# Attention value products over groups of two neighbouring query blocks, six probability places, scores two groups ahead

## Chip, core and metric

The kernel runs on one core of a Trainium2 chip (trn2). The metric is the device time of the whole program in microseconds (us), the median of three runs. The engines of a core run side by side and meet at semaphores: TensorE (PE) multiplies into PSUM, VectorE (DVE), ScalarE (ACT) and GpSimd (POOL) work element by element, SyncE (SP) issues DMAs.

## What is computed

One layer of a decoder trunk on 1024 tokens of width 1024, all float32. Four causal attention branches (A windowed, B dilated, C top-k, D forgetting), eight heads of 64 each, run on one input; each is projected, gated and summed, an output projection and a LayerNorm follow, then a convolutional gated FFN. The change lies in the attention proper, which in every branch has this form:

```python
s = einsum('bqhd,bshd->bhqs', q, k) * hd ** -0.5 + bias   # bias, slopes and masks differ by branch
p = softmax(where(causal, s, NEG_INF), axis=-1)           # branch A: a sink logit joins the denominator
o = einsum('bhqs,bshd->bqhd', p, v)
x = layer_norm(alpha * x + sum_branches(gate * proj(o)) @ w_out)
x = layer_norm(alpha * x + (gelu(conv(x @ w_up)) * (x @ w_ffn_gate)) @ w_down)
```

## The kernel before

Products are kept accurate by splitting an operand into a high and a low part (`hi`, `lo`, type fp32r), so a projection is three matmuls of 128x512 for each tile of weights and a value product is two (`pt_hi`, `pt_lo`).

The branches run in the order B, A, C, D, each as four pairs of heads. In a pair, 16 **units** (one head, one block of 128 queries) go through one chain. Unit (e, i) has i+1 key blocks of 128 (in A at most two). The chain of a unit is:

1. PE `scores`: two matmuls per piece of up to 512 columns into one of two `pair` buffers.
2. DVE `biased`: adds the bias, writes the probability place `prob_slot`, and takes the row's extreme.
3. ACT `exps`: exponential in place, with the row sum; in A one more small exponential for the sink.
4. DVE `inverse`: reciprocal of the sum (in A an addition before it).
5. POOL: scales the place by it.
6. PE `transposes`: 128x128 each, up to four into one of two `chunk` buffers; ACT `pt_hi`, then DVE `pt_lo` copy the chunk out as two parts, and free it.
7. PE `values`: for each key block two matmuls of 128 columns (the stationary operand is the block of v, the moving one the transposed probabilities), added up in a bank of `obank`; four units fill a bank, and ACT and DVE copy it out (`outputs`).

The order is written out by hand on every engine, by one loop over the units: at step u, PE does scores of unit u+2, transposes of u-1 and values of u-2; ACT does `pt` of u-2 and then `exps` of u; DVE `pt` of u-2, `biased` of u+1, `inverse` of u. `UNIT_ORDER` mixes long and short units. There are four probability places.

The **filler** is the projection of the next pair (q and k in B and D, q alone in A and C, the first gate tile of the merge at a branch's last pair). It is cut into parts of six matmuls, and PE takes parts of it only in the last five steps of a pair (u of 13 and more), between transposes and values; what is left follows after the loop. In A and C the next pair's q then goes through `place_q` (two ACT and two DVE instructions on 1024 columns) before its first scores (`chain`). In B, D and the first pair of A, v of the pair itself is projected ahead of the loop (`beside_v`): the first two units' scores run in that time, v is transposed, and ACT and DVE copy it out (`v_hi`, `v_lo`).

POOL also makes the low parts of weight tiles (`split_weights`, L1050), and up to two of them stand inside a pair, behind units 8 and 12.

Of the kernel before, what the change touches and what calls it, by code (L numbers as in the profile page):

```python
# [16 lines left out]
P = 128  # L43
# [38 lines left out]
PROB_SLOTS = 4  # L82
# [26 lines left out]
UNIT_ORDER = [(0, 0), (0, 1), (0, 2), (1, 7), (0, 3), (1, 6), (0, 4), (1, 5), (0, 5), (1, 4), (0, 6), (1, 3), (0, 7), (1, 2), (1, 1), (1, 0)]  # L109
# [16 lines left out]

_groups = [(e, i // 4) for e, i in UNIT_ORDER]
BANK_OF = [sorted(set(_groups), key=_groups.index).index(g) for g in _groups]  # L130
# [9 lines left out]
def begun(br, pr):  # L140


    return 2 if beside_v(br, pr) else 1 if pr > 0 else 0


def chunk_bases(br, pr, start):


    out = []
    for u, unit in enumerate(units_of(br, pr)):  # L150
        out.append(start)
        start += len(pieces(unit[4])) + (2 if u == 0 and beside_v(br, pr) else 0)
    return out
# [31 lines left out]
def build_layer(nc, x, w_in, b_forget, sinks, w_branch, w_gate, b_gate, w_out, ln1_g, ln1_b,  # L185
# [10 lines left out]
    with ctx:  # L196
# [11 lines left out]
        stat = sb("stat", [P, 64])  # L208

# [4 lines left out]
        prob = sb("prob", [P, PROB_SLOTS - 1, SEQ], F32, mixer)  # L214
        pt_hi = sb("pt_hi", [P, PT_SLOTS, HALF], F32R, mixer)
        pt_lo = sb("pt_lo", [P, PT_SLOTS, HALF], F32R, mixer)
        bias = sb("bias", [P, SEQ], F32, mixer)
        dist = sb("dist", [P, SEQ], F32, mixer)
# [89 lines left out]
        def prob_slot(br, u):  # L308

            k = u % PROB_SLOTS  # L310
            if k < PROB_SLOTS - 1:
                return prob[:, k, :]
            return {A: bias[:, HALF:SEQ], B: mid[:, 4, :], C: bias[:, :], D: score[:, 0:SEQ]}[br]
# [74 lines left out]
        def _(pe):  # L388
# [77 lines left out]
            def attention(br, pr, filler):  # L466
                units = units_of(br, pr)
                chain = br in (A, C) and pr < PAIRS - 1

                def transposes(u):  # L470
                    n = units[u][4]
                    pe.wait_ge(prob_ready, probs.next())
                    for s, m in pieces(n):
                        t = next_chunk()
                        for j in range(m // P):
                            last = nc.tensor.transpose(t[:, j * P:(j + 1) * P],  # L476
                                                       prob_slot(br, u)[:, s + j * P:s + (j + 1) * P], ident[:])
                        last.then_inc(chunk_full, 1)

                def values(u):  # L480
                    h, e, i, k0, n = units[u]
                    kv = {A: h // 4, C: 0}.get(br, e)
                    if BANK_EDGE[u][0]:
# [3 lines left out]
                    dst = obank[BANK_OF[u] % 2][:, (i % 4) * P:(i % 4 + 1) * P]  # L487
                    nkb = n // P
                    for s, m in pieces(n):
                        c = pvs.next() - 1  # L490
                        pe.wait_ge(chunk_free, chunk_base[u] + s // HALF + 1)
                        for j in range(m // P):
                            kb = s // P + j
                            v = v_view1[:, k0 + kb, :] if br == C else v_view[:, k0 + kb, kv, :]
                            for w, part in enumerate((pt_hi, pt_lo)):
                                last = nc.tensor.matmul(dst, v, part[:, c % PT_SLOTS, j * P:(j + 1) * P],  # L496
                                                        start=(kb == 0 and w == 0),
                                                        stop=(kb == nkb - 1 and w == 1))
                        if s + m < n or not BANK_EDGE[u][1]:
                            last.then_inc(pv_used, 1)  # L500
                        else:
                            last.then_inc(obank_full, 1)
# [7 lines left out]
                if beside_v(br, pr):  # L510
                    scores(br, pr, 2)
                    transposes(0)
                    pe.wait_ge(pair_free, pairs.n - 1)
                    transpose_tokens(staged)
                elif pr == 0:
                    pe.wait_ge(pair_free, pairs.n)
                    scores(br, pr, 0)
                    scores(br, pr, 1)
                n_units = len(units)
                for u in range(n_units + 2):  # L520
                    if u + 2 < n_units and not (u == 0 and beside_v(br, pr)):
                        scores(br, pr, u + 2)
                    draining = (2 if chain else 1) if u >= n_units - 3 else 0
                    if 1 + beside_v(br, pr) <= u <= n_units:
                        transposes(u - 1)
                    fill(draining)
                    if u == 2:
                        pe.wait_ge(chunk_free, chunk_base[1])
                    if u == n_units and chain:
# [3 lines left out]
                    if u >= 2:  # L533
                        values(u - 2)
# [223 lines left out]
        def _(act):  # L758
# [55 lines left out]
            def exps(br, pr, u):  # L814
# [3 lines left out]
                else:  # L818
                    act.wait_ge(pair_free, pairs.next())
                last = nc.scalar.activation(prob_slot(br, u)[:, 0:n], prob_slot(br, u)[:, 0:n], ACT.Exp,  # L820
                                            bias=stat[:, u % 4:u % 4 + 1], scale=-1.0,
                                            accum_out=stat[:, 4 + u % 4:5 + u % 4])
                if br == A:
# [11 lines left out]
            def attention(br, pr):  # L835
# [12 lines left out]
                def outputs(u):  # L848
                    if not BANK_EDGE[u][1]:
                        return  # L850
# [748 lines left out]
```

## Time and profile before

| | before |
|---|---|
| median of 3 runs | 2539.01 us (2538.95 to 2539.84) |
| profiled execution, span from first to last instruction | 2535.9 us |
| four pairs of B, first to last value product | 260.6 us |
| four pairs of A | 165.9 us |
| four pairs of C | 205.6 us |
| four pairs of D | 259.7 us |

The span and the median differ by 3.1 us, which lies around the first and last instruction. In the rows below a group of instructions reads: line, engine, operation, what it writes and reads, shape, count, then busy us, mean ns of one, idle time before. A timeline row reads: start, duration, engine, line, operation, and in brackets the idle time before it and who ended it. PE's durations overlap, so the time that a matmul takes from the stream is the distance of its start to the next one's start.

### The profile page before, as it was taken

The page shows a single profiled execution, that of the slowest core. Times are in us where ns is not written, and L with a number is a line of the kernel's source. Part 1 is how long each engine was busy: PE and PEld are TensorE (multiplying, and loading weights), DVE is VectorE, ACT ScalarE, POOL GpSimd, SP SyncE. Part 2 cuts the span into 40 slices and gives each one's busy share as a digit, 9 for nine tenths or more (in the row PEclk, how much of TensorE's full clock was granted, in tenths as well). Part 3 has the DMA queues.
Part 4 walks back from the last instruction along what each step waited for, and adds up shares of the span by engine and source line. Part 5 has one row for each costly group of instructions (what it writes and reads, how often), then busy time and mean ns, then how long its engine had stood idle before and what let it go on. Part 6 is the DMA issues. An engine that isn't in the chain of part 4 may idle for free. (4 is left out here: it accounts for less than half of the span.)

```text
span 2535.9 us, 30015 instructions
## 1 busy us (share of the span) xinstructions
PE 2352.2 (93%) x11696; PEld 1962.3 (77%) x11696; DVE 1231.5 (49%) x2359; ACT 868.9 (34%) x1533; POOL 629.8 (25%) x472
## 2 busy tenths in 40 slices
PE   7799999997889979899999999989999999999996
PEld 5488788786777767788888888868888888878775
DVE  3576556876568884551255553155211111134653
ACT  3355444125441144551155543232211112222331
POOL 1032222212212222222223222330122222224333
PEclk9799999998789989899999999999999999999998
DMA  3200001110001100001211001240111111123223
GB/s 108 19 26 17 18 22 38 40 52 17 13 18 46 50 15 7 9 18 50 71 34 42 26 23 54 79 137 1 42 45 47 50 50 51 50 67 100 86 88 108
DMA packets 165965, 116.33 MB, mean 46 GB/s; under 512 B 22456, under 2 KB 154552, under 8 KB 165824
## 3 DMA queue, kind: packets, MB, share of 16 engines
q1 hardware_dynamic: 149632, 112.21, 14.9%
q10 hardware_dynamic: 16192, 2.20, 0.6%
q8 instruction: 93, 1.52, 0.3%
q14 instruction: 48, 0.39, 0.1%
HBM read 110.17 MB, written 4.23 MB: 45 GB/s over the span
## 5 line engine op out<-in xcount | busy, mean ns | idle before, releaser
L1050 POOL TENSOR_TENSOR w_lo<-w_raw,w_hi 128x1024 fp32r<-128x1024 f32 (+1 forms) x190 | 425.3, 2239 | 1245.6 <-ACT w_hi L772 1245.6
L428 PE MATMUL pair<-act_hi,w_hi 128*128 128x512 f32 x1824 | 722.9, 396 | 12.4 <-DVE act_lo L1331 6.9
L428 PE MATMUL pair<-act_lo,w_hi 128*128 128x512 f32 x1824 | 713.3, 391 | 0.0
L428 PE MATMUL pair<-act_hi,w_lo 128*128 128x512 f32 x1824 | 713.1, 391 | 0.0
L772 ACT ACTIVATE w_hi<-w_raw 128x1024 fp32r<-128x1024 f32 (+1 forms) x190 | 187.3, 986 | 885.6 <-PE pair L428 703.5
L428 PEld LDWEIGHTS pair<-act_hi,w_hi 128*128 128x128 f32 x1824 | 344.5, 189 | 84.8 <-issue 8.5
L428 PEld LDWEIGHTS pair<-act_hi,w_lo 128*128 128x128 f32 x1824 | 344.2, 189 | 73.2
L428 PEld LDWEIGHTS pair<-act_lo,w_hi 128*128 128x128 f32 x1824 | 344.8, 189 | 67.4
L1273 DVE TENSOR_TENSOR pt_lo<-chunk,pt_hi 128x512 fp32r<-128x512 f32 (+3 forms) x352 | 182.0, 529 | 192.8 <-ACT pt_hi L792 189.8
L496 PE MATMUL obank<-pt_hi,heads 128*128 128x128 f32 x984 | 247.2, 288 | 5.8 <-DVE pt_lo L1273 5.7
L1079 POOL TENSOR_SCALAR prob<-prob,stat 128x896 f32<-128x896 f32 (+2 forms) x192 | 128.8, 671 | 471.9 <-DVE stat L1252 471.0
L496 PE MATMUL obank<-pt_lo,heads 128*128 128x128 f32 x984 | 243.9, 285 | 0.0
L792 ACT ACTIVATE pt_hi<-chunk 128x512 fp32r<-128x512 f32 (+3 forms) x352 | 161.4, 468 | 221.5 <-PE chunk L476 188.3
L451 PE MATMUL pair<-heads 128*128 128x512 f32 (+3 forms) x374 | 158.8, 425 | 54.9 <-DVE stat L1239 18.8
L496 PEld LDWEIGHTS obank<-pt_hi,heads 128*128 128x128 f32 x984 | 197.2, 200 | 12.9 <-DVE pt_lo L1273 8.0
L496 PEld LDWEIGHTS obank<-pt_lo,heads 128*128 128x128 f32 x984 | 198.1, 201 | 2.6
L1511 DVE SCALAR_TENSOR_TENSOR conv_s<-pair,convw,conv_s 128x1023 f32<-128x1023 f32 (+1 forms) x44 | 56.4, 1283 | 260.1 <-ACT conv_s L792 259.4
L428 PE MATMUL pair<-heads,w_hi 128*128 128x512 f32 x512 | 159.6, 393 | 13.3 <-DVE heads L1331 5.7
L1144 DVE TENSOR_SCALAR_CACHE_REDUCE o_top<-score,stat 128x640 uint8<-128x640 f32 (+3 forms) x182 | 162.2, 949 | 9.5 <-issue 8.4
L820 ACT ACTIVATE prob<-prob,stat 128x896 f32<-128x896 f32 (+2 forms) x192 | 133.4, 695 | 61.5 <-DVE stat L1239 60.8
L451 PEld LDWEIGHTS pair<-heads 128*128 128x128 f32 x374 | 82.3, 220 | 77.9 <-DVE stat L1239 26.6
L452 PE MATMUL pair<-heads 128*128 128x512 f32 (+3 forms) x374 | 137.6, 379 | 0.0
(190 smaller groups left out, 2958.5 us busy)
## 6 DMA issues: line engine op xcount, KB each, us to landing
w_raw<-in_w_down SPq DMA_DIRECT2D x44, 512.0 KB, 3.6
w_raw<-in_w_in SPq DMA_DIRECT2D x37, 512.0 KB, 3.8
w_raw<-in_w_gate SPq DMA_DIRECT2D x32, 512.0 KB, 4.1
w_raw<-in_w_up SPq DMA_DIRECT2D x22, 512.0 KB, 3.9
w_raw<-in_w_ffn_gate SPq DMA_DIRECT2D x22, 512.0 KB, 3.8
mid<-in_x SPq DMA_DIRECT2D x16, 512.0 KB, 6.7
w_raw<-in_w_branch SPq DMA_DIRECT2D x32, 256.0 KB, 2.8
w_raw<-in_w_out SPq DMA_DIRECT2D x8, 512.0 KB, 3.5
```

Of the source, the lines that this page charges most:

```text
L428: last = nc.tensor.matmul(dst[0:cols, s:s + HALF], w[:, k, :], a[:, k, s:s + HALF], start=(k == 0 and n == 0), stop=(k == kt - 1 and n == 2))
L451: nc.tensor.matmul(dst[:, s:s + m], q, k_hi[:, s:s + m], start=True, stop=False)
L452: last = nc.tensor.matmul(dst[:, s:s + m], q, k_lo[:, s:s + m], start=False, stop=not masked)
L496: last = nc.tensor.matmul(dst, v, part[:, c % PT_SLOTS, j * P:(j + 1) * P], start=(kb == 0 and w == 0), stop=(kb == nkb - 1 and w == 1))
L772: nc.scalar.activation(split_into(0, g), w_raw[:, g % 2, 0:kt * cols], ACT.Copy).then_inc(hi_ready, 1)
L792: nc.scalar.activation(dst, src, func, **kw).then_inc(act_part, 1)
L820: last = nc.scalar.activation(prob_slot(br, u)[:, 0:n], prob_slot(br, u)[:, 0:n], ACT.Exp, bias=stat[:, u % 4:u % 4 + 1], scale=-1.0, accu ...
L1050: nc.gpsimd.tensor_tensor(split_into(1, g), w_raw[:, g % 2, 0:kt * cols], split_into(0, g).bitcast(F32), ALU.subtract).then_inc(lo_ready, 1)
L1079: nc.gpsimd.tensor_scalar(prob_slot(step[1], u)[:, 0:n], prob_slot(step[1], u)[:, 0:n], stat[:, 12 + u % 4:13 + u % 4], 1.0, ALU.mult, ALU ...
L1144: nc.vector.tensor_scalar(junk[topk_where[0]][:, b % 2, 0:(i + 1) * P], s, limit if isinstance(limit, float) else limit[:, b:b + 1], None, ...
L1273: nc.vector.tensor_tensor(pt_lo[:, c % PT_SLOTS, 0:m], t[:, 0:m], pt_hi[:, c % PT_SLOTS, 0:m].bitcast(F32), ALU.subtract).then_inc(chunk_f ...
L1511: ins = nc.vector.scalar_tensor_tensor(conv_s[:, back:SEQ], src[:, 0:SEQ - back], convw[:, NCONV - 1 - back, ft:ft + 1], conv_s[:, back:SE ...
```

## The change

The 16 units become eight **groups** of two neighbouring query blocks 2m and 2m+1 of one head, in the order of `GROUPS`. One step g of the loop is now one chunk of a group. A chunk of B, C and D holds two key blocks for both query blocks (512 columns), and a group's last one 384; a group has m+1 chunks. In A every group has one chunk. The moving operand of a value product is 256 columns where both query blocks see the key block, and 128 for the last one (in A for two of the three). `exps` signals, and `inverse` and the first transposes wait, once for a group, that is for both its units. Scores of group j+2 go ahead at the first chunk of group j. Probability places are six, taken from spare memory (`aux`, `mid`, `score`). The filler starts with the seventh group (`j >= NGROUPS - 2`). POOL's splits still stand behind units 8 and 12.

```diff
-UNIT_ORDER = [(0, 0), (0, 1), (0, 2), (1, 7), (0, 3), (1, 6), (0, 4), (1, 5), (0, 5), (1, 4), (0, 6), (1, 3), (0, 7), (1, 2), (1, 1), (1, 0)]
+GROUPS = [(0, 0), (0, 1), (0, 2), (0, 3), (1, 2), (1, 1), (1, 3), (1, 0)]
+NGROUPS = len(GROUPS)
+UNIT_ORDER = [(e, 2 * m + w) for e, m in GROUPS for w in range(2)]
...
+def group_chunks(branch, j):
+
+    m = GROUPS[j][1]
+    if branch == A:
+        return [[(2 * m, (0, 1))] + [(2 * m - 1, (0,))] * (m > 0) + [(2 * m + 1, (1,))]]
+    blocks = [(kb, (0, 1)) for kb in range(2 * m + 1)] + [(2 * m + 1, (1,))]
+    return [blocks[c:c + 2] for c in range(0, len(blocks), 2)]
...
+                for g in range(len(stream) + 2):
+                    j, c = stream[g] if g < len(stream) else (NGROUPS, 1)
+                    ahead = c == 0 and j + 2 < NGROUPS
+                    draining = (2 if chain else 1) if j >= NGROUPS - 2 else 0
+                    if ahead:
+                        scores(br, pr, 2 * j + 4)
+                    if j < NGROUPS and not (g == 0 and beside_v(br, pr)):
+                        transposes(j, c)
                     fill(draining)
+                    if ahead:
+                        scores(br, pr, 2 * j + 5)
...
+                    if g >= 2:
+                        values(*stream[g - 2])
                     fill(draining)
```

ACT and DVE in the loop:

```diff
 # ACT
+                    if j < NGROUPS and not (g == 0 and beside_v(br, pr)):
+                        pt(j, c)
+                    if second is not None:
+                        exps(br, pr, second)
+                        second = None
+                    if c == 0 and j + 2 < NGROUPS:
+                        exps(br, pr, 2 * j + 4)
+                        second = 2 * j + 5
 # DVE
+                    if ahead:
+                        biased(br, pr, 2 * j + 4, chunk_base)
+                    if j < NGROUPS and not (g == 0 and beside_v(br, pr)):
+                        pt(j, c)
+                    if waiting is not None:
+                        inverse(br, waiting)
+                        waiting = None
+                    if ahead:
+                        biased(br, pr, 2 * j + 5, chunk_base)
+                        waiting = j + 2
 # POOL
+                        if u % 2 == 0:
+                            pool.wait_ge(rsum_ready, sums.next())
...
                         if u in (8, 12) and ring.n < needed + 2:
                             split_weights()
```

What stands in a row on POOL at the end of a pair of B, before (the scalings of units 11 and 12, a weight tile's low part, the scalings of 13 to 15):

```order
L1079 TENSOR_SCALAR mid<-mid,stat 128x512
L1079 TENSOR_SCALAR prob<-prob,stat 128x1024
L1050 TENSOR_TENSOR w_lo<-w_raw,w_hi 128x1024
L1079 TENSOR_SCALAR prob<-prob,stat 128x384
L1079 TENSOR_SCALAR prob<-prob,stat 128x256
L1079 TENSOR_SCALAR mid<-mid,stat 128x128
```

And in the changed kernel (units 10 and 11, unit 12, the low part, unit 13, units 14 and 15):

```order
L1112 TENSOR_SCALAR mid<-mid,att 128x384
L1112 TENSOR_SCALAR mid<-mid,att 128x512
L1112 TENSOR_SCALAR prob<-prob,att 128x896
L1082 TENSOR_TENSOR w_lo<-w_raw,w_hi 128x1024
L1112 TENSOR_SCALAR prob<-prob,att 128x1024
L1112 TENSOR_SCALAR mid<-mid,att 128x128
L1112 TENSOR_SCALAR prob<-prob,att 128x256
```

The low part stood between two units; it now stands between the two halves of the seventh group, of which PE's next transposes need both.

On ACT in the middle of a pair of A, before (`pt_hi` of a unit, exponential and sink of the unit two further):

```order
L792 ACTIVATE pt_hi<-chunk 128x256 [waits pv_used,chunk_full]
L820 ACTIVATE bias,stat<-bias,stat 128x256 [waits pair_free]
L824 ACTIVATE stat<-sink,stat 128x1
L792 ACTIVATE pt_hi<-chunk 128x256 [waits obank_full,chunk_full]
L820 ACTIVATE prob,stat<-prob,stat 128x256 [waits pair_free]
```

And now (`pt_hi` of group j, the second exponential of group j+1 with the sink, the first of group j+2):

```order
L816 ACTIVATE pt_hi<-chunk 128x512 [waits obank_full,chunk_full]
L844 ACTIVATE prob,att<-prob,att 128x256 [waits pair_free]
L848 ACTIVATE att<-att,sink 128x2
L844 ACTIVATE prob,att<-prob,att 128x256 [waits pair_free]
L816 ACTIVATE pt_hi<-chunk 128x512 [waits obank_full,chunk_full]
```

The exponential that completes a group now stands behind the `pt_hi` of the group just ahead of it; before, one unit lay between them.

## Rows read from the trace of the kernel before

**Rows 1.** Page, busy us of each engine (share of the span) xinstructions

```profile
PE 2352.2 (93%) x11696; PEld 1962.3 (77%) x11696; DVE 1231.5 (49%) x2359; ACT 868.9 (34%) x1533; POOL 629.8 (25%) x472
```

**Rows 2.** Stages B, A, C, D: us, busy PE, PEld, DVE, ACT, POOL, PEclk, DMA, GB/s

```profile
155.10:415.70 260.60, 247.97 (x1549) 216.45 (x1548) 154.10 (x345) 133.49 (x269) 71.71 (x73) 0.99 0.08 21
579.70:745.60 165.90, 137.69 (x670) 117.23 (x669) 94.11 (x336) 83.60 (x275) 39.43 (x67) 0.77 0.05 14
919.00:1124.60 205.60, 188.46 (x1235) 166.55 (x1235) 118.79 (x302) 111.57 (x245) 57.48 (x67) 0.93 0.04 11
1285.70:1545.40 259.70, 251.02 (x1607) 216.61 (x1606) 142.06 (x331) 133.91 (x268) 71.77 (x73) 1.00 0.11 33
```

**Rows 3.** Groups by line and shape, whole span, the value products

```profile
L496 PE MATMUL obank<-pt_hi,heads 128*128 128x128 f32 x984 | 247.2, 288 | 5.8 <-DVE pt_lo L1273 5.7
```

**Rows 4.** Timeline of PE in a pair of B

```profile
162.66 0.28 PE L496 MATMUL obank<-pt_hi,heads 128*128 128x128 f32 x1
162.78 0.28 PE L496 MATMUL obank<-pt_lo,heads 128*128 128x128 f32 x1
...
163.17 0.39 PE L452 MATMUL pair<-heads 128*128 128x512 f32 x1
163.40 0.28 PE L451 MATMUL pair<-heads 128*128 128x256 f32 x1
163.51 0.28 PE L452 MATMUL pair<-heads 128*128 128x256 f32 x1
163.64 0.82 PE L476 MATMUL chunk<-ident,prob 128*128 128x128 f32 x6
```

**Rows 5.** Timeline at the start of a pair of B, behind v

```profile
224.63 1.29 DVE L1331 TENSOR_TENSOR heads<-chunk,heads 128x512 fp32r<-128x512 f32 x2 [1.25 <-ACT heads L792]
...
226.44 0.50 PE L451 MATMUL pair<-heads 128*128 128x512 f32 x1 [1.19 <-DVE stat L1239]
```

**Rows 6.** Timeline at the end of a pair of B, one long unit and the split

```profile
248.42 1.22 DVE L1239 CUSTOM_DVE_ANT_0 prob<-pair,bias 128x1024 f32<-128x1024 f32 x1
...
250.68 1.14 ACT L820 ACTIVATE prob<-prob,stat 128x1024 f32<-128x1024 f32 x1
...
252.20 1.12 POOL L1079 TENSOR_SCALAR prob<-prob,stat 128x1024 f32<-128x1024 f32 x1 [1.70 <-DVE stat L1252]
...
253.28 2.40 POOL L1050 TENSOR_TENSOR w_lo<-w_raw,w_hi 128x1024 fp32r<-128x1024 f32 x1
253.38 1.18 PE L476 MATMUL chunk<-ident,prob 128*128 128x128 f32 x8 [0.41 <-POOL prob L1079]
```

**Rows 7.** Timeline in a pair of A, one turn of the chain

```profile
637.07 0.44 PE L476 MATMUL chunk<-ident,prob 128*128 128x128 f32 x2 [1.99 <-POOL prob L1079]
...
637.55 0.38 ACT L792 ACTIVATE pt_hi<-chunk 128x256 fp32r<-128x256 f32 x1 [2.06 <-PE chunk L476]
...
637.83 0.50 ACT L820 ACTIVATE bias<-bias,stat 128x256 f32<-128x256 f32 x1
...
638.32 0.28 ACT L824 ACTIVATE stat<-sink,stat 128x1 f32<-128x1 f32 x1
...
639.22 0.48 POOL L1079 TENSOR_SCALAR bias<-bias,stat 128x256 f32<-128x256 f32 x1 [1.20 <-DVE stat L1252]
```

**Rows 8.** Stretch of a pair of A, first transposes to filler

```profile
622.30:642.00 19.70, 16.70 (x93) 14.35 (x92) 16.03 (x64) 13.70 (x51) 8.05 (x13) 0.76 0.05 14
```

**Rows 9.** Timeline in C, the next pair's q is placed

```profile
1014.84 2.06 ACT L792 ACTIVATE heads<-pair 64x1024 fp32r<-64x1024 f32 x2 [6.46 <-PE pair L428]
...
1018.47 0.28 PEld L451 LDWEIGHTS pair<-heads 128*128 128x128 f32 x1 [2.89 <-DVE heads L1260]
```

**Rows 10.** Stretch of a pair of C, first scores to filler

```profile
964.60:1000.40 35.80, 32.55 (x227) 29.08 (x228) 25.70 (x69) 22.75 (x53) 12.83 (x14) 0.90 0.03 9
```

**Rows 11.** Two stretches in B behind each other

```profile
293.90:297.30 3.40, 0.66 (x6) 0.66 (x7) 2.68 (x8) 0.81 (x2) 0.00 (x0) 1.00 0.00 0
297.30:300.70 3.40, 3.15 (x10) 2.14 (x9) 2.60 (x5) 1.90 (x4) 0.00 (x0) 0.50 0.00 0
```

More of the change, by code:

```diff
@@ L81 @@
 PT_SLOTS = 3
-PROB_SLOTS = 4
+PROB_SLOTS = 3
 V_PARTS, MERGE_PARTS, FIRST_PARTS = 2, 13, 9
@@ L140, in begun @@
 def begun(br, pr):
-    return 2 if beside_v(br, pr) else 1 if pr > 0 else 0
+    return 2 if beside_v(br, pr) or pr > 0 else 0
 def chunk_bases(br, pr, start):
     out = []
-    for u, unit in enumerate(units_of(br, pr)):
+    for j in range(NGROUPS):
         out.append(start)
-        start += len(pieces(unit[4])) + (2 if u == 0 and beside_v(br, pr) else 0)
+        start += len(group_chunks(br, j)) + (2 if j == 0 and beside_v(br, pr) else 0)
     return out
@@ L468, in attention, with transposes, values @@
                 chain = br in (A, C) and pr < PAIRS - 1
[L470 to L481, printed above, removed]
+                stream = chunk_stream(br)
+                def transposes(j, c):
+                    if c == 0:
+                        pe.wait_ge(prob_ready, probs.next(2))
+                    t = next_chunk()
+                    at = 0
+                    for kb, halves in group_chunks(br, j)[c]:
+                        for w in halves:
+                            s = (kb - units[2 * j + w][3]) * P
+                            last = nc.tensor.transpose(t[:, at:at + P], prob_slot(br, 2 * j + w)[:, s:s + P], ident[:])
+                            at += P
+                    last.then_inc(chunk_full, 1)
+                def values(j, c):
+                    h, e, i, k0, n = units[2 * j]
                     kv = {A: h // 4, C: 0}.get(br, e)
-                    if BANK_EDGE[u][0]:
+                    chunks_of = group_chunks(br, j)
+                    if c == 0 and BANK_EDGE[j][0]:
                         o = obanks.next() - 1
@@ L1305, in attention @@
                             biased(br, pr + 1, 0)
-                    if u == len(units) - 1 and br in (A, C) and pr < PAIRS - 1:
-                        place_q(br, pr + 1)
-                    if u >= 3:
-                        outputs(u - 3)
-                outputs(len(units) - 1)
+                            biased(br, pr + 1, 1)
+                            waiting = 0
+                    if g >= 3 and bank_closes(br, *stream[g - 3]):
+                        outputs(stream[g - 3][0])
             def make_bias(br, pr):
```

251 lines of the change are left out of this document (133 added, 118 removed).

## The prediction

> **What bounds the kernel now.** I read the page's busy times first, then the stretches of the four attention stages, then the timeline of a pair in each. PE is the bound nearly everywhere: it is busy 93% of the span, DVE 49%, ACT 34% [rows 1]. In the attention stages the distance is smaller. PE is busy 248 of 261 us in B, 251 of 260 in D, 188 of 206 in C, but 138 of 166 in A, where its clock is granted at 0.77 on average, while DVE has 94 and ACT 84 us to do [rows 2]. So B, C and D go by the length of PE's stream, and A partly by the chain between the engines. Two questions decide: how much shorter the stream gets, and what PE then waits for.
>
> **Part 1, wider value products.** In the stream a value product of 128 columns takes 0.11 us, start to start (162.66 to 162.78) [rows 4]; its duration in the group, 288 ns, overlaps with its neighbours. There are 984 of each part, 1968 in all [rows 3]: 144 in a pair of B, C or D, 60 in a pair of A. The trace has no value product of 256 columns, but a score product of 256 columns with weights of its own takes 0.11 to 0.13 us (163.40, 163.51, 163.64) [rows 4]; I take 0.12. A pair of B, C or D will have 64 such and 16 of 128 columns: 64 x 0.12 + 16 x 0.112 = 9.5 us in place of 144 x 0.112 = 16.1, so -6.6. A pair of A has 16 and 28: 5.1 in place of 6.7, so -1.6. Over twelve and four pairs that is **-86 us of PE's stream**. At 0.11 it would be -94, at 0.13 -78.
>
> Against this stands a rule of the Trainium skill (TensorE: Matmul & The Clock Gate, section on what overlaps and what doesn't): a weight load overlaps a running matmul only where their row groups differ, which they don't here. The trace disagrees for wide products: one of 512 columns takes 0.23 us (163.17 to 163.40) [rows 4], four times the 0.055 that is left of 0.11 once half of it is the load. By the rule a product of 256 would cost 0.055 + 0.11 = 0.17, and the -86 would be -44; that is a rival below.
>
> **Part 2, fewer and fuller chunks.** A pair of B, C or D has 20 chunks in place of 24, one of A 8 in place of 16, and half as many signals. DVE and ACT save about 1 us a pair each; they are not the bound by their sums (half of PE's in the stage), so I cost this at nothing by itself. It is in the walks below.
>
> **Part 3, the chain is now one of groups.** This is where the gain goes. I walked the changed order by hand, with each engine's instructions in a row at the durations of the trace. Eight blocks take DVE's bias 1.22, ACT's exponential 1.14 and POOL's scaling 1.12 us [rows 6], the sum's read-out 0.19 more; shorter ones proportionally less, over a fixed part of some 0.2; a full chunk 0.5 on ACT and 0.6 on DVE, a hop between engines about 0.1.
>
> *Start of a pair of B or D.* Now PE waits 1.2 us for the bias behind the copies of v [rows 5]. After, the scores of unit 5 need unit 3's bias, which stands behind the same copies: about 1.7. Then the second group needs both its units scaled (0.8 of waiting), and the third again (1.5: it waits for unit 5's exponential, its reciprocal, and two scalings of 0.8 and 0.9 in a row). In the middle about 1.5 more, in pieces, where a chunk buffer is still being copied.
>
> *Before the filler.* Now the split of a weight tile, 2.40 us on POOL, costs PE 0.41: the transposes of unit 12 run beside it [rows 6]. After, it stands between units 12 and 13, which the seventh group needs both. Unit 13's scores end at t; DVE's bias is ready at t + 1.9 (a chunk is ahead of it), the exponential at t + 3.1, the reciprocal at t + 3.3; POOL adds 0.1 + 1.0 + 2.4 + 1.1, so the transposes start at t + 8.0. PE has only 5.0 us of work until then, and the filler stands behind these transposes: **3.0 us of waiting**, of which 2.4 are the split.
>
> Sum for such a pair: -6.6, and waits of 8.5 in place of 2.6, so -0.7; by absolute times of the walk -1.0, which I take. At a branch's last pair the filler is over with the eighth group's first chunk to come, and the copy of the outputs, 3 us on ACT, stands ahead of the last two banks: +1. Six pairs at -1 and two at +1: **-4**. If none of the new waits came, it would be -53; if each were half as long again, +19.
>
> *C.* The walk from a pair's first scores to the filler gives 31.1 us (14.1 to the third group's transposes, 17.0 from there; in C POOL has one split, not two) in place of 35.8 [rows 10]. But the filler of q is over two steps into the seventh group, and `place_q` stands behind the eighth group's `pt` on ACT; its 3.6 us from ACT's start to the next scores [rows 9] then have 0.5 us of PE's work beside them. From the filler's start to the next scores it is 19.4 in place of 18.1 (1018.47 [rows 9] less 1000.40 [rows 10]). **-3.4 for three pairs, -1 for the last: -11.**
>
> *A.* Every group has one chunk, so the chain closes on itself: PE transposes group j, ACT copies it, *then* runs the last exponential and the sink of group j+1, DVE adds and inverts, POOL scales two units, PE transposes j+1. From the timeline [rows 7]: first transpose to ACT 0.48 plus two more transposes 0.22; a full chunk 0.50; exponential to sink 0.49; sink 0.28; sink's end to POOL 0.62 (639.22 less 638.60) of which 0.1 is DVE's queue; two scalings 0.94; PE 0.06. That is **3.5 us for a group**. Now the same loop goes over two units, 2.9 us, with one scaling and a shorter copy: twelve units and the split take 19.7 us with the first step of filler [rows 8]. After, six groups take 6 x 3.5 + 2.4 = 23.4. PE's 1.6 us are saved beside it, where they are worth nothing. +4 for three pairs, +1 for the last, +3 for the first: **+16**.
>
> **The clock.** Where PE waited 3 us, the next 3.4 us ran at 0.50, that is 1.2 GHz in place of 2.4 [rows 11]; shorter waits were followed by that only sometimes. The new wait of 3.0 us ahead of the filler stands in each of the eight pairs of B and D, and the filler behind it is dense: 1.7 us lost each, taken for most of them, **+10**, from 0 up to +25 if the starts fall too.
>
> Sum: -4 - 11 + 16 + 10 = +11 us on the profiled 2535.9, and the same on the median, 3.1 us higher: **2550 us**. My walks share their errors across twelve pairs; one of 1 us in each is 12 us.
>
> **Rivals.**
> 1. *The run-ahead covers the starts and the middle.* Scores two groups ahead and six places are made for it, and DVE and ACT are far from full. Then B and D keep their old waits plus the split (-6.6 + 2.4, eight times -34), C loses only 1 us at `place_q` (-22), A stays at +16: 2539 - 40 = 2499. Halfway there is 2520. Against it: the three waits at the start follow from the order, not from load.
> 2. *PE stays the bound everywhere*, A too: 2539 - 86 = 2453. It would need A's loop not to close, which the order on ACT shows it does.
> 3. *The clock holds* in B and D: 2540, no change to be told.
> 4. *A load isn't hidden beside 256 columns.* Behind a narrow product the first wide one may take 0.17. The 832 wide ones would then cost 0.05 more each, 42 us, of which about half falls into waits: 2550 + 20 = 2570. By that rule of the skill this holds for all; the 512-column pace speaks against it.
> 5. *The clock falls in the starts as well*, and stays down over A: 2550 + 20 = 2570.
>
> **How the numbers follow.** Forecast (2540 to 2562 by itself) 0.38; rival 3 0.17; rival 1 0.17 and halfway 0.14; rival 2 0.04; rivals 4 and 5 0.05 each. A change within 0.2% (5 us) can't be told from none. Faster: 0.17 + 0.14 + 0.04 = 0.35. Same: rival 3 and the forecast's lower edge, 0.19. Slower: 0.46. The range leaves out rival 2, the faster half of rival 1 and the upper end of 4 and 5: 2500 to 2575.
>
> **What would show it.** Right: value products of 256 columns 0.12 us apart; PE waiting about 3 us for POOL ahead of the first filler part in each pair of B and D, with POOL's split just before; A's transposes 3.5 us apart, its stage about 180 us at a lower clock than 0.77; C about 195 us; B and D within 5 us of 261 and 260. Wrong: B and D each 15 us shorter or more (rival 1), A not longer (then the loop doesn't close), the wide products 0.17 apart (rival 4), the clock of B and D still at 0.99 and 1.00 (rival 3). PREDICTED's sign hangs above all on A and on the wait at POOL's split.

## The result and the profile after

The changed kernel takes **2603.98 us** (2597.4 to 2606.9, four runs), the kernel before in the same comparison 2539.43: a ratio of **1.0249, 95% interval 1.0231 to 1.0267**. I had forecast 2550 with a range up to 2575: slower was right, the size was not, 64 us in place of 11.

The page of the kernel after, busy us of each engine, and the four stages, first to last value product, in the columns of [rows 2] (us, busy PE, PEld, DVE, ACT, POOL, then PEclk, the granted share of TensorE's full clock):

```profile
PE 2318.0 (89%) x10864; PEld 1908.3 (73%) x10864; DVE 1213.5 (47%) x2120; ACT 855.7 (33%) x1421; POOL 626.7 (24%) x472
```

```profile
158.60:424.10 265.50, 226.56 (x1273) 191.46 (x1271) 147.22 (x287) 128.19 (x245) 69.43 (x71) 0.97 0.08 21
...
600.10:786.20 186.10, 134.18 (x581) 116.72 (x581) 72.87 (x227) 69.76 (x200) 36.72 (x63) 0.64 0.04 12
...
965.80:1161.00 195.20, 161.82 (x960) 139.25 (x958) 112.77 (x244) 105.70 (x221) 55.51 (x65) 0.92 0.04 12
...
1331.90:1606.00 274.10, 238.77 (x1329) 198.07 (x1327) 135.03 (x273) 128.05 (x245) 69.45 (x71) 0.94 0.11 31
```

Against [rows 1, 2]: PE is 34 us less busy and the span 69 us longer. B went from 260.6 to 265.5, A from 165.9 to 186.1, C from 205.6 to 195.2, D from 259.7 to 274.1. That is +29 in the stages, the smaller part of the loss: of the other 40 us one half lies ahead of a stage's first value product, which has fallen back by 4 to 7 us more than the projection ahead of it, and the other half behind its last. Stages bounded by value products were therefore a bad ruler. A better one: both kernels run the same 6240 projection matmuls in the same order, so the start of each in one trace less its start in the other says how far behind the changed kernel is at that point. Read at the landmarks of every pair, the 69 us fall into these pieces (sums over the pairs; -0.5 is left, ahead of the first):

| piece of the program | count | forecast, us | measured, us |
|---|---|---|---|
| B and D: end of v (or k) to the first filler matmul | 8 | -6 | -11.3 |
| B and D: first filler matmul to the projection of v | 6 | +10 (clock) | +30.7 |
| B and D: the projection of v | 6 | 0 | +6.3 |
| last pairs of B, C, D: first filler matmul to the end of the merge (in D to the FFN) | 3 | +2 | +21.4 |
| A: end of v to the last pair's filler | 4 | +16 | +29.3 |
| C: to the last pair's filler, with the merge before it | 4 | -11 | -7.0 |

The value products are what they were taken for. Timeline of PE in a pair of B, and the groups by shape:

```profile
251.58 0.28 PE L511 MATMUL obank<-pt_hi,heads 128*128 128x256 f32 x1
251.70 0.28 PE L511 MATMUL obank<-pt_lo,heads 128*128 128x256 f32 x1
251.81 0.28 PE L511 MATMUL obank<-pt_hi,heads 128*128 128x256 f32 x1
251.93 0.28 PE L511 MATMUL obank<-pt_lo,heads 128*128 128x256 f32 x1
```

```profile
L511 PE MATMUL obank<-pt_hi,heads 128*128 128x256 f32 x416 | 127.4, 322 | 1.0 <-DVE pt_lo L1304 1.0
...
L511 PE MATMUL obank<-pt_lo,heads 128*128 128x128 f32 x152 | 47.2, 314 | 0.0
```

They start 0.12 us apart, as forecast, with 256 columns and a weight load of its own for each.

**The wait ahead of the filler is there too.** PE and POOL at the end of a pair of B:

```profile
253.09 0.27 PE L511 MATMUL obank<-pt_lo,heads 128*128 128x128 f32 x1
256.10 1.11 PE L490 MATMUL chunk<-ident,prob 128*128 128x128 f32 x4 [2.73 <-POOL prob L1112]
```

```profile
251.61 1.01 POOL L1112 TENSOR_SCALAR prob<-prob,att 128x896 f32<-128x896 f32 x1 [4.90 <-DVE att L1284]
252.59 2.36 POOL L1082 TENSOR_TENSOR w_lo<-w_raw,w_hi 128x1024 fp32r<-128x1024 f32 x1
254.92 1.12 POOL L1112 TENSOR_SCALAR prob<-prob,att 128x1024 f32<-128x1024 f32 x1
```

Start to start PE lost 2.90 us beyond the matmul's own 0.11 (3.0 forecast), and the same in D (2.89). That holds in six of the eight pairs. In the last pair of B and of D the tile that POOL splits there has 512 columns and takes 1.28 us; PE loses 1.8. The 3.4 us behind the wait ran at a mean clock of 0.59 (0.53 to 0.62 in the six pairs, 1.00 in the last pair of B), the stretch ahead at 0.92 (us, busy PE to POOL, PEclk as above):

```profile
253.00:256.60 3.60, 0.87 (x7) 0.72 (x6) 2.04 (x8) 1.47 (x5) 3.60 (x4) 0.92 0.13 18
256.60:260.00 3.40, 3.40 (x14) 2.88 (x13) 0.69 (x1) 0.60 (x1) 0.24 (x1) 0.59 0.48 140
```

**The wait that I had not seen** stands 30 us later, where the filler (q and k of the next pair) is over and v's projection begins. PE, ACT and POOL:

```profile
284.85 0.39 PE L439 MATMUL pair<-act_hi,w_lo 128*128 128x512 f32 x1
288.48 0.47 PE L439 MATMUL pair<-act_hi,w_hi 128*128 128x512 f32 x1 [3.24 <-POOL w_lo L1082]
```

```profile
282.47 0.59 ACT L816 ACTIVATE o_top<-obank 64x512 f32<-64x512 f32 x1 [2.63 <-PE obank L511]
282.96 2.06 ACT L816 ACTIVATE heads<-pair 64x1024 fp32r<-64x1024 f32 x2
284.92 1.04 ACT L796 ACTIVATE w_hi<-w_raw 128x1024 fp32r<-128x1024 f32 x1
```

```profile
286.04 2.34 POOL L1082 TENSOR_TENSOR w_lo<-w_raw,w_hi 128x1024 fp32r<-128x1024 f32 x1 [29.20 <-ACT w_hi L796]
```

Read from the bottom: PE needs v's weights, POOL makes their low part when ACT has made the high part, ACT makes that in `place_q` of the next pair, and `place_q` stands in ACT's order behind the copy of the last output bank, so behind the last value product. Before, the loop took fewer parts of the filler, and v's projection began 8.3 us behind the last value product, which covered the 6.3 us of that chain. Now the filler is taken in seven steps, two parts in each: 14 of its 16 parts, and 2.8 us are left. The wait of 3.4 us stands in all six pairs. In D it has a second price: the projection of v behind it begins at half clock and takes 2.2 us longer. Behind the same wait the first two pairs of B kept the full clock (third row; the wait ends at 288.48), so the wait alone does not settle it.

```profile
1382.80:1386.30 3.50, 0.42 (x2) 0.00 (x0) 1.84 (x3) 3.42 (x5) 2.28 (x1) 0.93 0.00 0
1386.30:1389.70 3.40, 3.24 (x8) 2.60 (x9) 3.37 (x3) 2.84 (x3) 0.06 (x1) 0.50 0.60 154
...
288.50:291.90 3.40, 3.40 (x15) 2.83 (x16) 3.36 (x4) 2.67 (x3) 0.00 (x0) 1.00 0.58 154
```

At a branch's end the same thing meets the merge: the outputs' projection has to wait 2.48 us for the copies of the last outputs (1.25 before the change), and the 3.4 us behind that run at 0.59 (1.00 before).

```profile
429.58 0.82 PE L439 MATMUL pair<-heads,w_hi 128*128 128x512 f32 x2 [2.48 <-DVE heads L1373]
```

**A's loop** turns in 3.89 us where 3.5 were forecast, and in 5.1 to 6.2 where POOL's split stands between a group's two scalings; in the second pair the clock is 0.50 from end to end of the loop. One turn, PE and POOL, and the stretch:

```profile
648.45 1.11 PE L490 MATMUL chunk<-ident,prob 128*128 128x128 f32 x4 [1.68 <-POOL prob L1112]
...
651.35 0.93 POOL L1112 TENSOR_SCALAR prob<-prob,att 128x256 f32<-128x256 f32 x2 [2.96 <-DVE att L1284]
...
652.34 1.11 PE L490 MATMUL chunk<-ident,prob 128*128 128x128 f32 x4 [1.92 <-POOL prob L1112]
```

```profile
649.00:672.00 23.00, 15.13 (x66) 13.68 (x65) 9.31 (x34) 9.80 (x33) 6.96 (x11) 0.50 0.04 11
```

### The profile page after: what moved, and what is told of

Read it like the earlier page. It is cut to its first block and busy times, and to the rows that moved or that the text cites. A ratio compares the mean times of both kernels' runs of the same rounds, so it can differ in the third digit from the quotient of the medians.

```text
span 2605.0 us, 27672 instructions
## 1 busy us (share of the span) xinstructions
PE 2318.0 (89%) x10864; PEld 1908.3 (73%) x10864; DVE 1213.5 (47%) x2120; ACT 855.7 (33%) x1421; POOL 626.7 (24%) x472
## 5 line engine op out<-in xcount | busy, mean ns | idle before, releaser
L439 PE MATMUL pair<-act_hi,w_hi 128*128 128x512 f32 x1824 | 732.3, 401 | 30.8 <-POOL w_lo L1082 19.5
L439 PE MATMUL pair<-act_lo,w_hi 128*128 128x512 f32 x1824 | 723.2, 396 | 0.0
L1304 DVE TENSOR_TENSOR pt_lo<-chunk,pt_hi 128x512 fp32r<-128x512 f32 (+1 forms) x272 | 173.0, 639 | 290.9 <-ACT pt_hi L816 277.5
L816 ACT ACTIVATE pt_hi<-chunk 128x512 fp32r<-128x512 f32 (+1 forms) x272 | 149.4, 549 | 307.2 <-PE chunk L490 304.5
L1112 POOL TENSOR_SCALAR prob<-prob,att 128x256 f32<-128x256 f32 (+4 forms) x172 | 114.8, 675 | 432.7 <-DVE att L1284 432.7
L490 PE MATMUL chunk<-ident,prob 128*128 128x128 f32 x660 | 128.9, 306 | 78.3 <-POOL prob L1112 59.0
L439 PE MATMUL pair<-heads,w_hi 128*128 128x512 f32 x512 | 165.9, 405 | 17.6 <-DVE heads L1373 10.6
L1553 DVE SCALAR_TENSOR_TENSOR conv_s<-pair,convw,conv_s 128x1023 f32<-128x1023 f32 (+1 forms) x44 | 56.4, 1282 | 260.5 <-ACT conv_s L816 259.7
L511 PE MATMUL obank<-pt_hi,heads 128*128 128x256 f32 (+1 forms) x568 | 162.0, 305 | 1.0 <-DVE pt_lo L1304 1.0
L490 PEld LDWEIGHTS chunk<-ident,prob 128*128 128x128 f32 x660 | 86.3, 155 | 99.8 <-POOL prob L1112 72.5
L511 PE MATMUL obank<-pt_lo,heads 128*128 128x256 f32 (+1 forms) x568 | 149.5, 298 | 0.0
L844 ACT ACTIVATE prob<-prob,att 128x256 f32<-128x256 f32 (+4 forms) x172 | 120.5, 700 | 81.8 <-DVE att L1272 77.4
```

Of the source, the lines that this page charges most:

```text
L439: last = nc.tensor.matmul(dst[0:cols, s:s + HALF], w[:, k, :], a[:, k, s:s + HALF], start=(k == 0 and n == 0), stop=(k == kt - 1 and n == 2))
L490: last = nc.tensor.transpose(t[:, at:at + P], prob_slot(br, 2 * j + w)[:, s:s + P], ident[:])
L511: last = nc.tensor.matmul(obank[BANK_OF[j] % 2][:, q0:q0 + width], v, part[:, slot, at:at + width], start=(c == 0 and b == 0 and w == 0), ...
L816: nc.scalar.activation(dst, src, func, **kw).then_inc(act_part, 1)
L1304: nc.vector.tensor_tensor(pt_lo[:, n % PT_SLOTS, 0:m], t[:, 0:m], pt_hi[:, n % PT_SLOTS, 0:m].bitcast(F32), ALU.subtract).then_inc(chunk_f ...
```

## Experiments

My theory after the comparison: three waits of their own, each set by the order of something that the change did not mean to touch, make the 64 us. They are the filler drained too early, POOL's split within a group, and in A the exponential behind the copy. The rivals: the waits hide one behind another and only move when one is taken away; and the wide products are worth less than their pace says. The edits are to the changed kernel (2604 us), or to it with the three edits where that is said, each run beside the kernel before. No run puts these orders into the kernel before.

**One filler part per step in B and D and in the last pairs of A and C** (PE; `chain` is true in the other pairs of A and C):

```diff
                         values(*stream[g - 2])
-                    fill(draining)
+                    fill(draining if chain else 0)
```

> The changed kernel with one edit: in B, D and the last pairs, PE takes one filler part per step of the loop in place of two, so seven of the 16 parts in the loop and nine after the last value product (12.4 us of PE work in place of 2.8). Theory (filler drained too early): the 3.4 us wait for POOL's w_lo ahead of the projection of v goes in all six pairs, -20, and with it the half clock of that projection in D (2.7 us in three pairs, -8): about 2576. Rival (two parts a step were needed as cover for the chunk copies): the last seven steps wait about 0.5 us more each in eight pairs, +28, and the total stays at 2604 or above. Rival (w_hi or w_lo is late for another reason, its raw tile): the 3.4 us stay, whatever the filler does, 2604.

Measured: **2563.67 us** (ratio 1.0101, 1.0086 to 1.0116), -40. The high part is now made while the filler still runs, the wait for `w_lo` is gone in all six pairs, and v follows without a gap:

```profile
271.59 0.59 ACT L816 ACTIVATE o_top<-obank 64x512 f32<-64x512 f32 x1 [1.25 <-PE obank L511]
273.03 2.07 ACT L816 ACTIVATE heads<-pair 64x1024 fp32r<-64x1024 f32 x2 [0.85 <-PE pair L439]
275.00 1.04 ACT L796 ACTIVATE w_hi<-w_raw 128x1024 fp32r<-128x1024 f32 x1
```

```profile
276.13 2.39 POOL L1082 TENSOR_TENSOR w_lo<-w_raw,w_hi 128x1024 fp32r<-128x1024 f32 x1 [21.52 <-ACT w_hi L796]
```

By the landmarks: -24 between filler and v, -6 in v's projection, and -16 at the three ends of branches, which I had not expected: there the gate's filler now also reaches behind the last value product and covers the copies (the wait of 2.48 us has become 0.16). The cover theory is out.

**POOL's splits behind whole groups:**

```diff
-                        if u in (8, 12) and ring.n < needed + 2:
+                        if u in (9, 13) and ring.n < needed + 2:
```

> The changed kernel with one edit: POOL's two splits of weight tiles inside a pair stand behind units 9 and 13 in place of 8 and 12, so behind whole groups. Theory (the split cut the seventh group in two): the wait ahead of the filler falls from 2.9 to 0.5 us in the eight pairs of B and D (-19), the clock holds at full in the filler (1.6 us each, -13), in A the split costs at most what it did (0 to -9): 2563 to 2572. Rival (the wait only moves, to the eighth group or to the weights of the second tile, 2.4 us later): within 5 us of 2604. Rival between (the wait goes, the clock falls all the same): 2585.

Measured: **2565.05 us** (1.0102, 1.0087 to 1.0117), -39. The transposes now wait for a copy of a chunk, not for POOL, the split runs beside the filler, and the filler runs at full clock (0.59 before the edit):

```profile
249.99 2.10 POOL L1112 TENSOR_SCALAR prob<-prob,att 128x896 f32<-128x896 f32 x2 [4.88 <-DVE att L1284]
252.06 2.39 POOL L1082 TENSOR_TENSOR w_lo<-w_raw,w_hi 128x1024 fp32r<-128x1024 f32 x1
```

```profile
252.54 0.63 PE L490 MATMUL chunk<-ident,prob 128*128 128x128 f32 x4 [0.79 <-DVE pt_lo L1304]
```

```profile
256.00:259.40 3.40, 3.40 (x20) 2.88 (x19) 0.69 (x1) 0.60 (x1) 0.00 (x0) 1.00 0.45 133
```

By the landmarks it gave 28 us in B and D, the wait and the clock together, 13 in A, and 4 in C and the merge before it (the two profiled executions are 46 us apart, the medians 39). The 13 are more than the 9 that I had put in A: no turn of A is over 3.9 us now behind a pair's first, where five had been 5.1 to 6.2 (10 us), and between the transposes of the last two groups, where filler lies, it is 1.1 us less in three pairs. The wait of 3.4 us ahead of v is untouched by this edit, yet v's projection came back by 5 us; either edit removes most of that.

**Exponential ahead of the copy, in A alone** (ACT; on DVE likewise addition and reciprocal ahead of `pt_lo`):

```diff
+                    if br == A and second is not None:
+                        exps(br, pr, second)
+                        second = None
                     if j < NGROUPS and not (g == 0 and beside_v(br, pr)):
                         pt(j, c)
```

> The changed kernel with one edit, in A alone: ACT runs the exponential (with the sink) that completes a group ahead of pt_hi of the group before it, and DVE the addition and reciprocal ahead of pt_lo. Theory (A's loop closes over one group because of that order): a group's period falls from 3.9 us (3.4 at full clock) to about 2.8, the sum of two exponentials, sink and copy on ACT with hops: six groups in four pairs, -26; with the clock back to 0.77 another -10. 2568 to 2580. Rival (POOL's two scalings with PE's transposes and the bias are the loop, not the order on ACT): A within 5 us of 186, total 2600 to 2604.

Measured: **2569.93 us** (1.0136, 1.0114 to 1.0157), -34, all of it in A. The turn shown is 2.65 us (the others are 1.6 to 3.5, or 3.8 to 5.7 beside POOL's split, but for the first of A), and A at a clock of 0.80 takes 151.7 us, less than before the change:

```profile
644.90 0.66 PE L490 MATMUL chunk<-ident,prob 128*128 128x128 f32 x4 [1.00 <-POOL prob L1115]
...
647.55 0.66 PE L490 MATMUL chunk<-ident,prob 128*128 128x128 f32 x4 [1.05 <-POOL prob L1115]
```

```profile
600.60:752.30 151.70, 114.38 (x581) 99.17 (x581) 76.04 (x227) 70.69 (x198) 36.65 (x63) 0.80 0.05 15
```

So A's loop was what the walk said, the order on ACT. What sets the turn that is left was not tested. In the one shown PE does wait for POOL, but POOL has waited 1.72 us for DVE, and ACT begins the chunk's copy at 645.99, as the sink's exponential ends, 0.4 us behind the transposes: that looks like ACT and DVE waiting for each other (bias, exponential, sink, the two copies), not like the scalings.

```profile
645.99 0.57 ACT L816 ACTIVATE pt_hi<-chunk 128x512 fp32r<-128x512 f32 x1
...
646.57 0.93 POOL L1115 TENSOR_SCALAR prob<-prob,att 128x256 f32<-128x256 f32 x2 [1.72 <-DVE att L1287]
```

**Narrow products in the changed kernel:**

```diff
+                            for x in range(0, width, P):
-                                                    part[:, slot, at:at + width],
+                                                        part[:, slot, at + x:at + x + P],
```

> The changed kernel with one edit: each value product of 256 columns is issued as two of 128 with the same weights, so 144 in a pair of B, C or D as in the kernel before, all else unchanged. My term for the width was 0.12 us per wide product against 0.224 for two narrow ones: +6.6 us of PE's stream in a pair of B, C, D and +1.6 in A, +86 in all, of which what falls into waits is hidden, about a third in B and D, more in A: 2655 to 2675. Rival (the load is not hidden beside 256 columns, 0.17 each): +44 of stream, 2625 to 2640. Rival (the changed kernel is bound by its chain, so the width is worth nothing): under 2615.

Measured: **2641.12 us** (1.0405, 1.0387 to 1.0424), +37. Start to start, with waits cut off at 0.25 us, the value products take 240 us of PE's stream here and 159 in the changed kernel, 238 in the kernel before. So the width shortens the stream by 81 us (86 forecast), and 44 of them fall into waits. The time came out below my 2655 to 2675, at the edge of the first rival's range, but that rival's cause is out: it wanted 44 us of stream. What I had too low was the share that falls into waits, half and not a third.

**The three edits together:**

> The changed kernel with the three edits of the runs before together: one filler part per step in B and D, POOL's splits behind whole groups, in A exponential and reciprocal ahead of the copies. Alone they gave -40, -39 and -34 us. Theory (three separate waits, none takes the other's place): nearly their sum, less what the first two share in the filler's clock and the last two in A: -95 to -110, 2494 to 2509, faster than the kernel before. Rival (one wait hides behind another, so a part of each was counted twice): -60 to -75, 2530 to 2545, no better than the kernel before.

Measured: **2493.34 us** (0.9819, 0.9804 to 0.9834), -111, nearly the sum of 40, 39 and 34. The three waits are separate, the rival is out, and the grouping with the three edits now beats the kernel before by 1.8%. Its stages (B, A, C, D):

```profile
158.20:402.40 244.20, 218.19 (x1267) 185.88 (x1266) 149.50 (x289) 130.23 (x247) 69.98 (x71) 1.00 0.08 22
573.00:714.40 141.40, 110.05 (x564) 95.91 (x563) 77.44 (x229) 71.11 (x200) 37.01 (x63) 0.78 0.06 16
898.10:1087.00 188.90, 156.59 (x956) 135.42 (x955) 115.29 (x246) 107.81 (x223) 55.71 (x65) 0.95 0.04 12
1253.70:1497.10 243.40, 223.42 (x1324) 187.81 (x1322) 137.79 (x275) 130.26 (x247) 69.91 (x71) 1.00 0.12 35
```

**The same with narrow products:**

> The kernel with the three edits, with each value product of 256 columns issued as two of 128. In the changed kernel the width was worth 37 us of the 86 of the stream. Theory (the rest fell into PE's waits): with the waits gone the width is worth more, 55 to 70 us on top of the kernel with the three edits. Rival (the other 49 us were never in the stream, a wide product costs more than 0.12): again 35 to 40.

Measured: **2531.01 us** (0.9974, 0.9962 to 0.9985), +38 on the three edits. My theory failed here: the width is worth no more with the waits gone. But the rival as I wrote it fails as well, since the stream is 78 us longer (228 against 151, counted as above). The third pair of D, up to the projection of v, shows where the rest is. The wide products take 6.7 us less there, at their usual pace, and the pair only 3.3. What PE loses beyond each matmul's usual pace is 9.1 us with wide products and 6.0 with narrow ones (5.0 before the change); of that the profile shows 5.1 and 3.1 as idle time, and waits for `pt_lo` are 2.2 and 0.4 of it, most of them in the long groups. PE in that pair with wide products:

```profile
1402.14 0.66 PE L490 MATMUL chunk<-ident,prob 128*128 128x128 f32 x4 [0.62 <-DVE pt_lo L1307]
1403.57 0.55 PE L490 MATMUL chunk<-ident,prob 128*128 128x128 f32 x3 [0.28 <-DVE pt_lo L1307]
...
1412.60 0.63 PE L490 MATMUL chunk<-ident,prob 128*128 128x128 f32 x4 [0.79 <-DVE pt_lo L1307]
```

With wide products PE is through a chunk before ACT and DVE have copied the next, so the width itself makes these waits. The run also splits the gain: of the 45 us below the kernel before, 38 are the width, and 7 the grouping and the three edits together.

**Keeping PE busy in A** (changed kernel; the real transposes overwrite the results):

```diff
+                    t = next_chunk()
+                    if br == A:
+                        for _ in range(8):
+                            nc.tensor.transpose(t[:, 0:P], ident[:], ident[:])
```

> The changed kernel with one addition: in A, PE does eight transposes of the identity into the chunk buffer of each group ahead of its wait for POOL (0.9 us at full clock; 32 groups, results overwritten by the real ones). Computation unchanged. A's loop is 3.9 us for a group with PE at 0.50. Theory (the half clock is a consequence of the waits and lengthens the loop by 0.4 to 0.5 us): the clock in A rises from 0.64 to over 0.85, A is 10 to 16 us shorter, 2588 to 2594. Rival (so little work does not raise the clock): granted clock within 0.05 of 0.64, and A as long or up to 15 us longer, as the eight transposes take 1.8 us at half clock where the wait was shorter than that.

Measured: **2608.03 us** (1.0270, 1.0255 to 1.0285): no gain, so the time of my theory failed, though its clock came. The clock did rise, from 0.64 to 0.87, and in the timeline a turn of the loop fell from 3.89 to 3.43 us, near the 3.5 that the walk had at full clock. A was only 5 us shorter: at a pair's start, where PE still ran at a low clock (0.60 over 7 us in the second pair), POOL's scalings of the second group came 7.19 us behind those of the first in place of 5.48, so the eight transposes cost there a good part of what the turns gave. Another 3.6 us were lost behind A, 1.2 in the merge and 2.4 in C, where nothing was edited. The same code of C took between 0.9 us less and 2.4 us more than in the changed kernel in three such runs; what makes it vary I don't know.

```profile
602.00:783.30 181.30, 136.66 (x814) 121.28 (x813) 72.47 (x227) 69.89 (x200) 36.70 (x63) 0.87 0.04 12
```

**Exponentials first in all branches** (the three edits, the third without its `br == A`):

> The kernel with the three edits, the third of them in all branches in place of A alone: the exponential that completes a group, and its reciprocal, stand ahead of the copies of the next chunk everywhere. Theory (the same order closes the loop in the short groups of B, C and D): the waits for POOL at the start of a pair fall by 0.5 to 1 us, -8 to -15 on the kernel with the three edits. Rival (in long groups the copy of a chunk now stands behind an exponential that waits for a bias of 1.2 us, and PE for the chunk): +5 to +20.

Measured: **2536.58 us** (0.9993, 0.9983 to 1.0002), +43 on the three edits: the rival, at twice its price, 2.5 to 4.8 us in a pair of B, C and D. PE waits for the copy of a chunk, which stands behind the exponential of a long unit, which waits for its bias (PE and ACT in D):

```profile
1356.90 1.15 ACT L844 ACTIVATE prob<-prob,att 128x1024 f32<-128x1024 f32 x1 [0.95 <-DVE att L1275]
...
1359.24 0.66 PE L490 MATMUL chunk<-ident,score 128*128 128x128 f32 x4 [0.68 <-DVE pt_lo L1307]
```

**Three small moves on top of the three edits,** and two of them together. The filler one step earlier; q of C in two parts per step; the order of the third edit at the second step of every pair:

```diff
-                    draining = (2 if chain else 1) if j >= NGROUPS - 2 else 0
+                    draining = (2 if chain else 1) if j >= NGROUPS - 2 or (j == NGROUPS - 3 and c == 1 and not chain) else 0
...
+                    draining = (2 if chain and br == A else 1) if j >= NGROUPS - 2 else 0
...
-                    if br == A and second is not None:
+                    if (br == A or g == 1) and second is not None:
```

> The kernel with the three edits, and in B, D and the last pairs the filler starts one step earlier, at the second chunk of the sixth group (one part more in the loop, eight left behind it). In the kernel with the three edits PE waits 0.95 us for pt_lo just ahead of the seventh group. Theory (the chain is 1 us late there, and a part of 1.4 us covers it): -0.95 in each of ten pairs, about -8 to -10, 2484 to 2486. Rival (the wait moves to the next chunk, or a part there delays values that free a copy place): within 3 us of 2493.

> The kernel with the three edits, and in C PE takes two filler parts per step in place of four, so that the eight parts of q reach over four steps. Theory (they cover the waits of 0.3 to 0.95 us for pt_lo in the steps behind, of some 2 us in a pair): -1.5 in three pairs, -4 to -6, 2488. Rival (q is then finished later, and place_q, 3.7 us of waiting now, comes as much later): 0 to +6.

> The kernel with the three edits, and outside A exponential and reciprocal ahead of the copies at the second step of a pair alone (the third group's). In all steps of B, C and D this cost 43 us. Theory (the order helps where groups are short and hurts only where the exponential waits for a bias of 1 us): the wait for POOL ahead of the third group falls by 0.4 to 0.6 us in twelve pairs, -4 to -7, 2486 to 2489. Rival (the order hurts there too, PE then waits for the second group's copy): +3 to +12, as a third or so of the 3.6 us that a pair lost when it was done in all steps.

> The kernel with the three edits, with q of C in two parts per step and the order of the second step of a pair (the two variants that were 2 to 3 us below it, each within the interval). Theory (both are real and independent): 2487 to 2489. Rival (both were noise): 2491 to 2495. Neither changes the verdict against the kernel before.

Measured: 2497.03 (0.9839, 0.9825 to 0.9853), 2491.60 (0.9818, 0.9805 to 0.9832), 2490.07 (0.9813, 0.9799 to 0.9828), and the last two together 2489.84 (0.9795, 0.9781 to 0.9808). The interval of each overlaps that of the three edits (0.9804 to 0.9834), that of the first and that of the pair together only at its edge. No theory's time came: -8 to -10, -4 to -6 and -4 to -7 were forecast, +3.7, -1.7 and -3.3 measured, and the pair lies between its theory and its rival. The first did what its rival said, and a little worse. The wait only moved: the 0.95 us for a copy became a wait for the bias of the last scores, ahead of the filler itself. And with one part of the filler less behind the last value product, a wait of 1.22 us for the copies of the outputs came back in each of the three merges, the changed kernel's fault again, in small.

```profile
1413.82 0.47 PE L439 MATMUL pair<-act_hi,w_hi 128*128 128x512 f32 x1 [0.60 <-DVE att L1275]
```

The third took the wait of 1.1 us for POOL away in D, and 0.8 us of waits for chunk copies came in its place: -0.4 in a pair. The waits that are left are tied to each other, unlike the three large ones.

## Point by point

- **Bound.** "B, C and D go by the length of PE's stream" was half true. It held before the change (PE idle for 2.3 of 60 us in a pair of D); the change itself made the chain the bound wherever a group needs both its units.
- **Part 1, -86 us of stream.** Right: 0.12 us for a product of 256 columns, 81 us by the narrow run. What the run adds is its worth in time: 37 us.
- **Part 2, chunks, 0.** Nothing measured speaks against it; no run took it alone.
- **Part 3, B and D.** The walk was good: 3.0 us ahead of the filler forecast, 2.9 measured in six pairs (1.8 in the two last, where the split tile is half as wide, which I had not seen); -6 us over the attention proper, measured -11.
- **The step that failed: where the filler ends.** I wrote of the last pairs that "the filler is over with the eighth group's first chunk to come", and for the six others I stopped the walk at the filler's start, "and the filler stands behind these transposes". I never followed it to its end, where the next consumer is v's projection, fed by ACT behind the last outputs and by POOL behind ACT. So the sum has nothing at all between the filler and v but the clock. That left out 3.4 us in six pairs and v's half clock (27 us by the landmarks less the clock term, 30 by the run), and at the ends of three branches 19 more than the +2 forecast, of which the run gave back 16.
- **A, +16.** The mechanism is right, and the run with the exponentials first shows it; the term was too small, 29. The 3.5 us of a turn are those of full clock; at the half clock that A fell to they are 3.9, and the pairs' starts and the filler ran below full clock too (0.70 and 0.84 in the second pair). I gave that to rival 5 at 20 us and a chance of 0.05.
- **C, -11.** Half of it came. -10.4 by value products only seems to agree, since C's first value product fell back by 5.5 us more than the projection ahead of it, so the stage began late. By the landmarks C itself gave 5.6 us, and the -7.0 of the table have 1.4 of the merge before it.
- **The clock, +10.** Filler's start to v is +30.7 less 20.4 of waiting, so +10, and with the split behind the group, where the filler ran at full clock, 8 of it went. The size is as forecast, but from six pairs and not eight. Rival 3 is out.
- **Rival 1** (the run-ahead covers the starts): out in the changed kernel. **Rival 4** (the load isn't hidden beside 256 columns): out; the Trainium skill's rule (TensorE: Matmul & The Clock Gate, section "What overlaps and what doesn't") does not hold for this stream: 0.12 us for 256 columns with a weight load every time, 0.11 for 128.

What was missing from the range: I added up errors of sizes, and left no room for a wait at a place that I had not walked.

## What to carry to other kernels

When an edit moves work that fills gaps, follow it to its end and ask who is fed behind it: the wait showed up 30 us after the code that was changed. When two units become one group, look at everything that stands between them on each engine, and put it behind the group. Compare two traces by instructions that both have in the same order, not by the stage's own first and last.

## What the runs showed of the hardware

A tiny addition on DVE waits for POOL's whole split. In the kernel before, DVE's addition of one column (both operands in SBUF) takes 0.16 us, but 2.25 when POOL's `w_lo` is running. In all five places where the two meet in that kernel it ends within 0.02 us of the split, whenever it began (the first two rows are of one stretch, the last is 5 us later):

```profile
633.87 2.36 POOL L1050 TENSOR_TENSOR w_lo<-w_raw,w_hi 128x1024 fp32r<-128x1024 f32 x1
...
633.99 2.25 DVE L1250 TENSOR_TENSOR stat<-stat 128x1 f32<-128x1 f32 x1
```

```profile
638.77 0.16 DVE L1250 TENSOR_TENSOR stat<-stat 128x1 f32<-128x1 f32 x1
```

In the kernel with the three edits it happens four times, in three of A's pairs (1.07 us at 660.40, where the split began at 659.09). It costs little there, since POOL's next scaling stands behind the split anyway. The Trainium skill (GPSIMD Engine Reference, section "Specifications") says that the two engines contend for SBUF where the DVE instruction has two SBUF inputs; the trace agrees, and shows the size: not a slower instruction, but one that is held to the other's end.

The clock goes with PE's waits, but not wait by wait. Behind the wait of 2.9 us ahead of the filler 3.4 us ran at 0.53 to 0.62 in all six pairs; behind the wait of 3.4 us ahead of v it was 0.50 in three pairs, 0.71 in one and 1.00 in two. Eight useless transposes in each of A's waits brought A from 0.64 to 0.87. But the clock is worth little where the stretch goes by other engines: 0.5 us of a turn of 3.9.
